# Gate products of a linear recurrence as 64x64 matmuls on the four quarters of the PE array, in a two-block fp32 transformer kernel

## What is computed

```python
def rg_lru(u, w_rg, b_rg, w_ig, b_ig, lam):
    ub = u.reshape(B, S, N_LRU_BLOCKS, LRU_BLOCK)          # 8 blocks of 64 channels
    r = jax.nn.sigmoid(jnp.einsum('bsnc,ncd->bsnd', ub, w_rg) + b_rg)
    i = jax.nn.sigmoid(jnp.einsum('bsnc,ncd->bsnd', ub, w_ig) + b_ig)
    log_a = -LRU_C * r * jax.nn.softplus(-lam)
    a = jnp.exp(log_a)
    mult = jnp.sqrt(-jnp.expm1(2.0 * log_a))
    bterm = mult * (i * u)
    _, h = lax.associative_scan(_linear_rec_combine, (a, bterm), axis=1)   # h = a h + bterm
    return h
```

## Time and profile before

| what | value |
|---|---|
| median of 3 runs | 717.80 us |
| the profiled execution's own time | 717.69 us |
| its span, first to last instruction | 716.0 us |
| PE busy | 710.5 us (99%) |
| VectorE busy | 535.0 us (75%) |
| ScalarE busy | 424.2 us (59%) |
| POOL busy | 190.6 us (27%) |
| mean granted TensorE clock | 0.999 |

### The profile page before, as it was taken

How to read it: one execution, slowest core, us unless ns; L and a number is a source line. 1 busy time by engine, 2 the same in 40 slices (tenths; PEclk the granted TensorE clock), 3 DMA queues, 4 the chain that set the end, 5 groups by cost and what they waited for, 6 DMA issues and landing times.

```text
span 716.0 us, 9290 instructions
## 1 busy us (share of the span) xinstructions
PE 710.5 (99%) x3488; PEld 591.1 (83%) x3488; DVE 535.0 (75%) x715; ACT 424.2 (59%) x550; POOL 190.6 (27%) x128
## 2 busy tenths in 40 slices
PE   9999999999999999999999999999999999999998
PEld 7777878888888888888888888888889888888886
DVE  6899999999987665555556454678866577879997
ACT  7646676664893554444444255469845777865660
POOL 1298998989300030000000000144000134000000
PEclk9999999999999999999999999999999999999999
DMA  9877446455557556555665555633354565655541
GB/s 318 265 221 236 132 162 206 156 170 176 177 192 249 161 184 211 180 176 178 186 210 168 185 194 170 231 138 120 119 174 143 183 206 158 199 181 205 199 177 59
DMA packets 79739, 131.59 MB, mean 184 GB/s; under 512 B 4064, under 2 KB 37032, under 8 KB 79696
## 3 DMA queue, kind: packets, MB, share of 16 engines
q1 hardware_dynamic: 79008, 130.28, 55.0%
q10 hardware_dynamic: 544, 0.53, 0.2%
q0 software_dynamic: 144, 0.20, 0.1%
HBM read 129.75 MB, written 1.25 MB: 183 GB/s over the span
## 4 chain that ended last, share of the span: by engine, by line
PE 96%; DVE 1%; POOL 1%; DMA 1%; ACT 1%; issue 1%; SPq 0%; ACTq 0%
PE acc L1950 21%; PE acc L1952 21%; PE acc L1951 21%; PE aux L1906 4%; PE aux L1610 3%; PE acc L1906 3%; PE acc L1961 3%; PE acc L1962 3%; PE acc L1963 3%; PE aux L1912 2%; PE acc L1912 2%; PE aux L1962 1%; PE aux L1961 1%; PE aux L1963 1%; PE aux L1653 1%; PE aux L1671 1%
## 5 line engine op out<-in xcount | busy, mean ns | idle before, releaser
L1099 DVE TENSOR_TENSOR w_lo<-raw,w_hi 128x2048 fp32r<-128x2048 f32 (+1 forms) x96 | 215.2, 2246 | 86.3 <-ACT w_hi L745 86.3
L745 ACT ACTIVATE w_hi<-raw 128x2048 fp32r<-128x2048 f32 (+2 forms) x115 | 214.6, 1870 | 85.6 <-PE acc L1952 69.6
L1950 PE MATMUL acc<-w_hi,h_both 128*128 128x512 f32 x488 | 195.0, 400 | 0.4 <-DVE tok L1191 0.4
L1952 PE MATMUL acc<-w_hi,h_both 128*128 128x512 f32 x488 | 190.6, 391 | 0.0
L1951 PE MATMUL acc<-w_lo,h_both 128*128 128x512 f32 x488 | 190.1, 390 | 0.0
L1950 PEld LDWEIGHTS acc<-w_hi,h_both 128*128 128x128 f32 x488 | 91.7, 188 | 20.2 <-issue 1.4
L1952 PEld LDWEIGHTS acc<-w_hi,h_both 128*128 128x128 f32 x488 | 91.6, 188 | 19.7
L1951 PEld LDWEIGHTS acc<-w_lo,h_both 128*128 128x128 f32 x488 | 91.8, 188 | 17.7
L606 POOL TENSOR_TENSOR w_lo<-raw,w_hi 128x2048 fp32r<-128x2048 f32 x21 | 97.9, 4677 | 1.4 <-ACT w_hi L745 1.4
L1180 DVE SCALAR_TENSOR_TENSOR aux<-glu_t,vec_t,aux 128x256 f32<-128x256 f32 x232 | 93.6, 485 | 0.0
L629 POOL TENSOR_TENSOR rstd<-ms,nhalf 128x2 f32<-128x2 f32 x3 | 8.0, 2682 | 267.4 <-DVE ms L1161 256.5
(11 more groups left out here) (295 smaller groups left out, 1115.4 us busy)
## 6 DMA issues: line engine op xcount, KB each, us to landing
raw<-w_in_dram SPq DMA_DIRECT2D x29, 1024.0 KB, 5.2
raw<-w_down_dram SPq DMA_DIRECT2D x26, 1024.0 KB, 4.9
raw<-w_gate_up_dram SPq DMA_DIRECT2D x44, 512.0 KB, 4.8
raw<-w_up_dram SPq DMA_DIRECT2D x16, 1024.0 KB, 5.5
raw<-w_out_dram SPq DMA_DIRECT2D x8, 1024.0 KB, 5.1
raw<-w_in_dram SPq DMA_DIRECT2D x12, 512.0 KB, 4.7
raw<-w_proj_attn_dram SPq DMA_DIRECT2D x4, 1024.0 KB, 5.0
raw<-w_proj_conv_dram SPq DMA_DIRECT2D x4, 1024.0 KB, 5.0
```

Of the source, the lines that this page charges most:

```text
L745: ins = nc.scalar.activation(hi_cell(u)[:, part, :], src, ACT.Copy)
L1099: ins = nc.vector.tensor_tensor(lo_cell(u)[:, part, :], src, f(hi_cell(u)[:, part, :]), ALU.subtract)
L1950: nc.tensor.matmul(o, x_h, w_hi[:, slot, j, :], start=begin_, stop=False)
L1952: mm = nc.tensor.matmul(o, x_l, w_hi[:, slot, j, :], start=False, stop=end_)
```

## The change

The two 128x128 gate matmuls of each ct become four of 64x64, one on each quarter of the array (rows of u by columns of the output). The recurrence gate's blocks lie on the diagonal quarters. The input gate's lie on the other two, so its output halves land on the wrong 64 partitions, and ScalarE's sigmoid reads one half of the partitions and writes the other. Two ct share a pair of banks: one for each gate. So each ct has three sigmoids instead of two. The weights' tiles, their loads and their zeros are as before.

```diff
-        LRU_BANK = [0, 1, 3, 2]
+        LRU_BANK = [[0, 1], [3, 2]]
+        HALF = [slice(0, HD), slice(HD, P)]
+
+        def lru_part(ct, gate):
+
+            return aux[:, LRU_BANK[ct // 2][gate], S * (ct % 2):S * (ct % 2 + 1)]
...
                     if s == B + 6:
-                        act.wait_ge(ri_made, ct + 1)
-                        bank = LRU_BANK[ct]
-                        nc.scalar.activation(decay_gate[:, ct, :], aux[:, bank, 0:256], ACT.Sigmoid, bias=vcol(R_RG, ct))\
+                        act.wait_ge(ri_made, ct + 2 - ct % 2)
+                        nc.scalar.activation(decay_gate[:, ct, :], lru_part(ct, 0), ACT.Sigmoid, bias=vcol(R_RG, ct))\
                             .then_inc(ri_kept, 1)
-                        nc.scalar.activation(in_gate[:, ct, :], aux[:, bank, 256:512], ACT.Sigmoid, bias=vcol(R_IG, ct))\
-                            .then_inc(ri_kept, 1)
+                        for n in range(2):
+                            nc.scalar.activation(in_gate[HALF[n], ct, :], lru_part(ct, 1)[HALF[1 - n]], ACT.Sigmoid,
+                                                 bias=vcol(R_IG, ct)[HALF[n]]).then_inc(ri_kept, 1)
                 if s == B + 6:
                     act.wait_ge(coef_ready, 1)
-                    act.wait_ge(ri_kept, 2 * CT2)
+                    act.wait_ge(ri_kept, 3 * CT2)
...
                 if s == B + 6:
-                    dve.wait_ge(ri_kept, 2 * CT2)
+                    dve.wait_ge(ri_kept, 3 * CT2)
...
-                bank = LRU_BANK[ct]
-                claim([bank], ri_kept, 2 * ct + 2)
-                nc.tensor.matmul(aux[:, bank, 0:S], wr_g[:, ct, :], lru_u[:, ct, :], start=True, stop=True)
-                nc.tensor.matmul(aux[:, bank, S:2 * S], wi_g[:, ct, :], lru_u[:, ct, :], start=True, stop=True)\
-                    .then_inc(ri_made, 1)
+                if ct % 2 == 0:
+                    claim(LRU_BANK[ct // 2], ri_kept, 3 * ct + 6)
+                for rows in range(2):
+                    ps = HALF[rows]
+                    nc.tensor.matmul(lru_part(ct, 0)[ps], wr_g[ps, ct, ps], lru_u[ps, ct, :], start=True, stop=True,
+                                     skip_group_check=True)
+                    mm = nc.tensor.matmul(lru_part(ct, 1)[HALF[1 - rows]], wi_g[ps, ct, ps], lru_u[ps, ct, :],
+                                          start=True, stop=True, skip_group_check=True)
+                mm.then_inc(ri_made, 1)
```

## The result

The changed kernel takes **720.51 us** (median of 4 runs, 720.20 to 722.08) against 717.76 of the kernel before: ratio 1.0044, 95% interval 1.0032 to 1.0057. It is slower, as forecast, but the time lies 0.3 above the top of the range and 1.1 above the forecast.

What follows compares the result with a forecast made beforehand. PE, busy 710.5 of 716.0 us, was taken to bound the kernel. Gates −1.2, idle at k's turn +0.95 and at the suffixes +1.98 gave net +1.73 on 717.69, so 719.4 us; range 717.7 to 720.2.

Steps and rivals of the forecast that it cites:

- PE, the gates, gain 1.2: Gate matmuls on PE: quarters side by side take 2.2 us instead of 3.46, a gain of 1.2 us.
- rival C: Gate matmuls on PE: quarters run one after another, 3.7 us later, 721.4 us in all; chance 0.04.
- 0.25 left at k's turn, because L1191 is late: PE at k's turn: VectorE's L1191 comes no earlier, so 0.25 of 1.2 us remains and PE idles 0.95.
- Reading one half and writing the other is in no row. I price it at nothing: ScalarE's sigmoids: moving data between partition halves adds no cost of its own, 0 us.
- I take 1.43: ScalarE's sigmoids: four more at 0.36 each add 1.43 us, ending the exps at 489.92.
- 4 × 0.52 = 2.1: ScalarE's sigmoids: upper bound for the four added ones, with no overlap at all, 2.1 us.
- POOL ahead of L1527: VectorE against POOL: POOL's second L600 comes first at 490.92 and holds L1527, which ends 2.68 us later, at 493.94.
- The suffixes +1.73: PE's first suffixes: they start at 503.48 instead of 501.75, 1.73 us later, and nothing is given back behind.
- Rival D: ScalarE or PE's clock: moved halves cost more, or longer idle time lowers PE's clock; 720.1 us, chance 0.04.
- Rival B: VectorE against POOL: L1527 goes before POOL's L600, so not slower; 718.0 us, chance 0.30.
- Slower at 0.60, the rest at "same": Whole kernel: chance 0.60 of slower by over 0.2% (above 719.2 us), 0.38 same, 0.02 faster.

Runs made afterwards that it cites:

- experiment 1: Changed kernel with two full sigmoids per channel tile, nothing moved between halves (input gate left exchanged): 717.27 us, ratio 0.9992 to the kernel before.
- experiment 9: Kernel before plus quarters, DMA copy of u with halves exchanged, eight full sigmoids, and squares of k ahead of unit B+8's high part: 716.85 us, ratio 0.9988.
- experiment 3: Kernel before, its matmuls kept, with three sigmoids per channel tile, input gate in two halves each kept on its partitions: 721.14 us, ratio 1.0049.
- experiment 4: Changed kernel with its twelve sigmoids grouped by partitions (four full, four of one half, four of the other): 720.56 us, ratio 1.004 to the kernel before.
- experiment 7: Version with quarters, DMA-crossed copy of u and eight full sigmoids (717.4), plus seven extra tanh on ScalarE: 720.52 us, ratio 1.0045 to the kernel before.

## Why the prediction was wrong

- **PE, the gates, gain 1.2:** right, 1.05 to 1.1 measured, in the changed kernel and in experiment 1. So was the dismissal of rival C. Four quarters run side by side, and the first records of four calls start before the second record of any, so the gates did not stay at the 3.5 us of strict program order. Channel tile 2 waited for the copy of q, as reckoned: it starts at 476.67, 0.47 behind tile 1's last records instead of 0.22.
- **0.25 left at k's turn, because L1191 is late:** right, 0.24 in experiment 1. In the changed kernel the lead shrinks there from 1.18 to 0.41 (net from 1.05 to 0.28), so 0.77 are lost where the forecast had 0.95, of which the profile charges only 0.4 to L1196. Its reason is shown by experiment 9, where an earlier L1201 lets the rest through.
- **"Reading one half and writing the other is in no row. I price it at nothing" and "I take 1.43":** this is the step that failed. Twelve sigmoids at 0.50 in place of eight at 0.36 put 2.9 us on ScalarE, not 1.43. The upper bound, 4 × 0.52 = 2.1, was no bound: it let only the four added instructions lose their overlap, while the eight that were there lost theirs too. With no overlap at all the bound would have been eleven steps of 0.50 against seven of 0.36, 3.0. The cause is the change of the first partition, not the move (experiments 3 and 4). That this delay makes the whole loss is shown by experiment 7.
- **POOL ahead of L1527:** the mechanism was right and the place wrong. ScalarE being 1.5 later than reckoned (net), POOL's 490.77 fell before the squaring, which was held for 1.25. Near the size that the forecast had for ScalarE it does hold the combination, as experiment 4 shows (and experiment 3).
- **The suffixes +1.73:** measured 2.8 net, before the clock fell. L1530 starts 1.5 later than forecast (net), the hold is 1.25 instead of 1.52, and PE follows L1217 by 0.05 instead of 0.14.
- **Rival D** named both of what went wrong, moved halves that cost more and a lower clock behind PE's idle time, with 0.04 and a time of 720.1. The clock adds 1.7 to the runs that it hits, where nothing was added for it.
- **Rival B**, the lower end of the range, needed POOL to come after the combination had begun. In neither trace of the changed kernel did it (490.77, and 491.03 in the second, with the squaring asked for at 491.29 and 491.56).
- **Slower at 0.60, the rest at "same":** the direction was right; the time, 720.51, is above the range because of the one term.

## What to carry to other kernels

If an edit cuts instructions of ScalarE into pieces, count the steps of all neighbours again, not only the added ones: pieces on alternating partitions take away the overlap of what stands around them, and grouping the pieces by partition gives it back. A gain on the engine that bounds the kernel is worth only what the next meeting point lets through. A delay on an engine that looks idle costs its length, plus the turn of another engine that it now has to wait for, less the slack in front of the bounding engine; here 2.9 us on ScalarE and a turn of POOL cost more than twice what PE had won. If data must change partitions, do it before the waited-for chain begins, where a DMA has time to land.

## What the hardware showed that was not expected

- ScalarE: ACTIVATEs of 128x256 or 64x256 from PSUM with a bias from a tile start 0.35 to 0.38 apart if source and destination keep their first partition, and 0.48 to 0.51 apart if either changes. Half the partitions with the other half as destination cost no more than that.
- TensorE's granted clock: in two traces it stood at about half (0.53 over 3.6 and 3.4 us) after a wait of 2.3 us in a PE that was otherwise busy. Of 26 runs of kernels with a wait of 2.1 to 2.3 us, nine had a mean clock of 0.997 or 0.998 and were 1.5 to 2.1 us longer than the median of the others of their kernel; of 63 runs of kernels with 1.8 us or less, none.
- TensorE: sixteen calls on four quarters, two records each, ran as eight rows of four records each, the starts of a row within 0.05 of each other, and a row 0.21 to 0.27 behind the one before where nothing was waited for; getting back to 128x128 cost 0.31 for the first step and 0.34 for the second, against 0.23.
